# One decoder layer with a mixture of experts: the last expert's rows normalised by themselves and scattered into the output

## What is computed

```
def hierarchical_moe(h, ...):
    ...                      # each token: top-1 group of 8 experts, then top-2 experts inside it
    def expert_block(args):
        xb, e = args
        hid = jax.nn.silu(xb @ w_gate[e]) * (xb @ w_up[e])
        return hid @ w_down[e]
    y = lax.map(expert_block, (x_rows, block_expert)).reshape(R, D)
    y = y * row_w[:, None]
    out = jax.ops.segment_sum(y, row_tok, num_segments=T + 1)[:T]
...
z = ALPHA * h + hierarchical_moe(h, ...)
out = layer_norm(z, ln2_scale, ln2_bias)     # mean and variance over the 2048 channels of a token
```

## Time and profile before

| | us |
|---|---|
| median of 3 executions | 2080.28 (2080.22 to 2081.01) |
| span of the profiled execution, first to last instruction | 2078.8 |
| median less that span | 1.5 |
| PE busy, DVE busy, ACT busy, POOL busy | 1783.7, 980.9, 766.0, 10.1 |

### The profile page before, as it was taken

How to read it: one execution, slowest core, us unless ns; L and a number is a source line. 1 busy time by engine, 2 the same in 40 slices (tenths; PEclk the granted TensorE clock), 3 DMA queues, 4 the chain that set the end, 5 groups by cost and what they waited for, 6 DMA issues and landing times.

```text
span 2078.8 us, 25166 instructions
## 1 busy us (share of the span) xinstructions
PE 1783.7 (86%) x9828; PEld 1156.3 (56%) x9828; DVE 980.9 (47%) x1428; ACT 766.0 (37%) x1332; POOL 10.1 (0%) x26
## 2 busy tenths in 40 slices
PE   9999999999999999999999986667666766666667
PEld 7888888888888888888888541112111211111122
DVE  6454454545444454566565564343443343334334
ACT  5444444344444444354443422222222222222222
POOL 0000000000000000000000000000000000000000
PEclk9999999999999999999999988888888887888889
DMA  7555545455555555467677999999999999999997
GB/s 248 192 176 178 185 153 177 160 187 178 197 183 171 162 180 164 162 189 240 216 274 291 383 428 426 428 430 431 427 430 430 432 429 427 429 430 431 427 429 324
DMA packets 138481, 615.16 MB, mean 296 GB/s; under 512 B 14080, under 2 KB 14752, under 8 KB 117408
## 3 DMA queue, kind: packets, MB, share of 16 engines
q1 hardware_dynamic: 138400, 614.02, 76.8%
HBM read 611.89 MB, written 2.10 MB: 295 GB/s over the span
## 4 chain that ended last, share of the span: by engine, by line
PE 61%; DMA 34%; DVE 2%; issue 1%; ACT 1%; SPq 0%; DVEq 0%; ACTq 0%
DMA W<-in_w_expert_up_dram 21%; PE PS L564 16%; PE PS L566 16%; PE PS L565 16%; DMA W<-in_w_expert_down_dram 13%; PE PS L1119 4%; PE PS L1165 2%; PE PS L866 1%; DVE WL L541 1%; PE PS L910 1%; PE PS L1238 1%; PE PS L890 0%; PE PS L1077 0%; ACT WH L537 0%; PE PS L854 0%
## 5 line engine op out<-in xcount | busy, mean ns | idle before, releaser
L541 DVE TENSOR_TENSOR WL<-RAW,WH 128x1024 fp32r<-128x1024 f32 x384 | 458.1, 1222 | 402.3 <-ACT WH L537 401.1
L537 ACT ACTIVATE WH<-RAW 128x1024 fp32r<-128x1024 f32 x384 | 394.3, 1058 | 251.3 <-PE PS L566 201.9
L564 PE MATMUL PS<-WH,XH 128*128 128x512 f32 x1216 | 485.2, 399 | 1.3 <-DVE WL L541 1.2
L566 PE MATMUL PS<-WH,XL 128*128 128x512 f32 x1216 | 474.6, 390 | 0.0
L565 PE MATMUL PS<-WL,XH 128*128 128x512 f32 x1216 | 473.7, 390 | 0.0
L1119 PE MATMUL PS<-W,XE 128*32 128x512 f32 x2016 | 279.0, 702 | 146.2 <-DMA W<-in_w_expert_up_dram 144.8
L1165 PE MATMUL PS<-W,HT 128*32 128x512 f32 x992 | 170.5, 849 | 132.1 <-DMA W<-in_w_expert_down_dram 132.1
L2150 DVE TENSOR_TENSOR ZACC<-PS,ZACC 128x1024 f32<-128x1024 f32 x116 | 136.6, 1220 | 290.2 <-PE PS L1207 290.2
L1119 PEld LDWEIGHTS PS<-W,XE 128*32 128x32 f32 x2016 | 71.9, 125 | 334.6 <-issue 200.3
L564 PEld LDWEIGHTS PS<-WH,XH 128*128 128x128 f32 x1216 | 228.4, 188 | 50.5 <-DVE WL L541 5.4
L566 PEld LDWEIGHTS PS<-WH,XL 128*128 128x128 f32 x1216 | 228.2, 188 | 49.0
(11 more groups left out here) (309 smaller groups left out, 1500.0 us busy)
## 6 DMA issues: line engine op xcount, KB each, us to landing
RAW<-in_w_in_dram SPq DMA_DIRECT2D x304, 512.0 KB, 4.6
W<-in_w_expert_gate_dram SPq DMA_DIRECT2D x62, 2048.0 KB, 28.6
W<-in_w_expert_up_dram SPq DMA_DIRECT2D x62, 2048.0 KB, 33.1
W<-in_w_expert_down_dram SPq DMA_DIRECT2D x29, 4096.0 KB, 35.2
RAW<-in_w_branch_ret_dram SPq DMA_DIRECT2D x32, 512.0 KB, 4.9
RAW<-in_w_out_dram SPq DMA_DIRECT2D x32, 512.0 KB, 5.7
W<-in_w_expert_down_dram SPq DMA_DIRECT2D x5, 2048.0 KB, 27.8
RAW<-in_w_branch_attn_dram SPq DMA_DIRECT2D x16, 512.0 KB, 5.2
```

Source lines behind the costliest of these rows:

```text
L537: act.activation(WH[:, i % RING], RAW[:, i % RING], ACT.Copy).then_inc(hi_done, 1)
L541: dve.tensor_tensor(WL[:, i % RING], RAW[:, i % RING], WH[:, i % RING].bitcast(F32), ALU.subtract).then_inc(lo_done, 1)
L564: pe.matmul(PS[:, bank + t], hs, wh, start=first and j == 0, stop=False)
L566: mm = pe.matmul(PS[:, bank + t], ls, wh, start=False, stop=end)
```

## The change

It does six things.

1. **Order of the last loads.** `LAST_PLACES` gives the last pieces buffers: down 30 into 0, first half of 31 into 1, second half of 31 into 2, down 31 into 3. Down 30 is now issued ahead of item 31's halves. The broadcast reads of scale and bias go; instead both are read as 32 rows of 128 values (`LN2R`, 8 KB each), early: behind `load_down(2, 2)`, after waits for `table_ready` and `s1_spread` 4.
2. **Order on PE.** Items 29 and 30 are spread and added to `ZACC` as all others. Behind item 30 PE runs `number_slots`, `gather_sums`, `spread_norm2(0)`, `spread_norm2(1)`, first half of item 31, `spread_norm2(2)`, `spread_norm2(3)`, second half of item 31, `spread_compact`, `turn_hidden(31)`, `down_last`, `join_stats`.
3. **All sums but item 31's are normalised and stored.** DVE runs `row_stats` on `ZACC` and `norm_rows(j)` for four quarters of 512 channels, with scale and bias spread by PE into PSUM (`spread_norm2`); SP stores `OB` in two DMAs of 1 MB behind the fourth.
4. **Item 31 stays compact.** `gather_sums` copies the sums of its rows out of `ZACC` into `XE_BANK`; `down_last` accumulates onto them, the row weight being in the hidden values already (`hidden_last`, `WHALF`).
5. **Its LayerNorm** is made on 128 partitions by 512: `bn_stats`, a matmul with `JOIN` that brings the four quarters of a row together, `bn_aggr`, `pow` on POOL and two DVE instructions.
6. **Its rows are scattered**: POOL waits for the stores of step 3 and issues one indirect DMA of 128 rows of 2 KB over them.

The core of the diff (declarations, the branches for `n_more`, and removed functions that the sections above name are left out):

```diff
+LAST_PLACES = {(2, NE - 2): 0, (0, NE - 1): 1, (1, NE - 1): 2, (2, NE - 1): 3}
...
         load_down(2, 2)
+        sp.wait_ge(table_ready, 1)
+        sp.wait_ge(s1_spread, 4)
+        for v, row in ((ln2_scale, 0), (ln2_bias, KD)):
+            sp.dma_start(LN2R[row:row + KD], v.rearrange("l (r n) -> (l r) n", n=P)).then_inc(s2_landed, 16)
...
+        sp.wait_ge(d_used, (NE - 2) * 2)
+        for c in range(2):
+            load_last(2, NE - 2, c)
+        sp.wait_ge(gu_used, (NE - 1) * GU + 2)
+        for c in range(2):
+            load_last(0, NE - 1, c)
         sp.wait_ge(gu_used, NE * GU)
+        for c in range(2):
+            load_last(1, NE - 1, c)
         sp.wait_ge(d_used, (NE - 1) * 2)
+        load_last(2, NE - 1, 0)
...
-        sp.dma_start(S2B[:], ln2_scale.broadcast_to((P, D))).then_inc(s2_landed, 16)
-        sp.dma_start(B2B[:], ln2_bias.broadcast_to((P, D))).then_inc(s2_landed, 16)
+        def store_rows(run):
+            sp.wait_ge(normed, 4 * run + 4)
+            for t in range(TOK):
+                sp.dma_start(out_rows[:, t], OB[:, t]).then_inc(stored, 16)
...
+        def gather_sums():
+            pe.wait_ge(xe_stored, NE * QS)
+            pe.wait_ge(added, (NE - 1) * 4 + 2)
+            for t in range(TOK):
+                for m in range(QD):
+                    pe.matmul(PS[m * ROWS:(m + 1) * ROWS, XE_BANK], SEL[:, t],
+                              ZACC[:, t, m * QC:(m + 1) * QC], start=t == 0, stop=False)
+        def number_slots():
+            pe.wait_ge(slots_ready, 1)
+            for m in range(QD):
+                for t in range(TOK):
+                    mm = pe.matmul(PS[m * ROWS:(m + 1) * ROWS, Y_BANK, 0:1], SEL[:, t], TOKV[:, t:t + 1], ...)
+        def spread_norm2(j, run=0):
+            pe.wait_ge(s2_landed, 32)
+            ...
+            if j >= 2:
+                pe.wait_ge(normed, 4 * run + j - 1)
+            for v in range(2):
+                for r in range(QD):
+                    row = v * KD + j * QD + r
+                    mm = pe.matmul(PS[:, norm_bank(j) + v, r * P:(r + 1) * P],
+                                   RC[0:2 * KD, R_ID + row:R_ID + row + 1].broadcast_to((2 * KD, P)), LN2R[0:2 * KD], ...)
+            mm.then_inc(s2_spread, 1)
+        def spread_compact():
+            pe.wait_ge(normed, 3)
+            for v in range(2):
+                for r in range(QD):
+                    row = v * KD + r
+                    for m in range(QD):
+                        col = R_ID + row + m * QD
+                        mm = pe.matmul(PS[m * ROWS:(m + 1) * ROWS, SPREAD + v, r * P:(r + 1) * P],
+                                       RC[0:2 * KD, col:col + 1].broadcast_to((2 * KD, ROWS)), LN2R[0:2 * KD], ...)
+            mm.then_inc(s2_spread, 1)
...
+        pe.wait_ge(h_ready, NE - 1)
         turn_hidden(NE - 2)
+        for t in range(TOK):
+            spread_rows(NE - 3, t)
+        down(NE - 2, 2, range(KH), halves=True)
+        for t in range(TOK):
+            spread_rows(NE - 2, t)
+        number_slots()
+        gather_sums()
+        spread_norm2(0)
+        spread_norm2(1)
+        gate_up(NE - 1, 3, 0, take(1), last=True)
+        spread_norm2(2)
+        spread_norm2(3)
+        gate_up(NE - 1, 3, 1, take(1), last=True)
+        spread_compact()
         turn_hidden(NE - 1)
         down_last()
+        join_stats()
...
+        def norm_rows(j, run):
+            cols = slice(j * CH, (j + 1) * CH)
+            dve.wait_ge(s2_spread, 5 * run + j + 1)
+            for t in range(TOK):
+                dve.scalar_tensor_tensor(OB[:, t, cols], ZACC[:, t, cols], MV2[:, t, 0:1], PS[:, norm_bank(j)], ...)
+            dve.wait_ge(c_rstd, run + 1)
+            dve.drain()
+            for t in range(TOK):
+                last = dve.scalar_tensor_tensor(OB[:, t, cols], OB[:, t, cols], RSTD2[:, t:t + 1],
+                                                PS[:, norm_bank(j) + 1], ALU.mult, ALU.add)
+            last.then_inc(normed, 1)
...
         row_weights(NE - 2)
+        add_rows(NE - 3, 1)
         row_tokens(NE - 2)
+        y_low(NE - 2)
+        add_rows(NE - 2, 0)
+        row_weights(NE - 1)
+        add_rows(NE - 2, 1)
+        row_tokens(NE - 1)
...
+        row_stats()
+        for j in range(3):
+            norm_rows(j, 0)
+        hidden_last()
+        norm_rows(3, 0)
+        dve.wait_ge(slots_summed, 1)
+        dve.tensor_tensor(IDX[:], PS[:, Y_BANK, 0:1], SLOT[:], ALU.add).then_inc(idx_ready, 1)
+        dve.wait_ge(last_summed, 1)
+        dve.bn_stats(BS3[:], PS[:, XE_BANK])
+        dve.drain()
+        dve.tensor_tensor(BSX[:], BS3[:, None, :].broadcast_to((P, QD, 6)), OWN[:], ALU.mult).then_inc(part_stats, 1)
+        dve.wait_ge(joined, 1)
+        dve.bn_aggr(MV3[:], PS[:, Y_BANK, 8:8 + 6 * QD])
...
+        rstd(MV2[:, :, 1], VE2[:], RSTD2[:], NHF[:], d_stats, 1, c_rstd)
+        pool.wait_ge(last_var, 1)
+        pool.tensor_tensor(RSTD3[:], VE3[:], NHF[:, 0:1], ALU.pow).then_inc(last_rstd, 1)
+        pool.wait_ge(idx_ready, 1)
+        pool.wait_ge(stored, 16 * TOK)
+        pool.wait_ge(last_done, 1)
+        pool.indirect_dma_start(out_slots, bass.IndirectOffsetOnAxis(ap=IDX[:, 0:1], axis=0), LZ[:], None, ...)
```

More of the change, by code:

```diff
@@ L1087, in turn_rows, with gate_up @@
             mm.then_inc(xe_turned, 1)
-        def gate_up(item, k4, q, rows, more=False, gathered_between=None):
+        def gate_up(item, k4, q, rows, more=False, gathered_between=None, last=False):
             by_place = isinstance(item, int) and item < 2 and q == 0
@@ L1093, in gate_up @@
                 pe.wait_ge(xe_stored, item * QS + (q + 1))
-            pair_q = MORE_PAIRS[q] if more else place(q, k4) % PAIRS
+            pair_q = MORE_PAIRS[q] if more else LAST_PLACES[q, item] if last else place(q, k4) % PAIRS
             apart = isinstance(item, int) and item == 0 and q == 1
@@ L1147, in down @@
         def down(item, k4, blocks, first=False, halves=False, more=False):
-            pair_q = MORE_PAIRS[2] if more else place(2, k4) % PAIRS
+            pair_q = MORE_PAIRS[2] if more else LAST_PLACES[2, item] if halves else place(2, k4) % PAIRS
             for b in blocks:
@@ L1198, in spread_rows @@
+        def spread_rows(item, t):
+            if t == 0:
                 pe.wait_ge(g_ready, item + 1)
                 pe.wait_ge(y_act, item + 1)
-            if not onto:
-                pe.wait_ge(added, item * 4 + 2 * (t != first) + 2)
+            pe.wait_ge(added, item * 4 + 2 * t + 2)
             for part, y in ((0, YH), (1, YL)):
-                if t == first and part == 1:
+                if t == 0 and part == 1:
                     pe.wait_ge(y_dve, item + 1)
@@ L1207, in spread_rows @@
                     mm = pe.matmul(PS[:, SPREAD + m], GS[rows, t * P:(t + 1) * P], y[rows, :],
-                                   start=part == 0 and not onto, stop=part == 1 and not onto)
+                                   start=part == 0, stop=part == 1)
                     if part == 1 and m % 2:
                         mm.then_inc(spread, 1)
-        def spread_last(item, t, n, of=(0, 1)):
-            last = item == NE - 1
-            gs, parts = (GSL, (YHL, YLL)) if last else (GS, (YH, YL))
-            for part in of:
-                for m in range(2):
-                    rows = slice((2 * n + m) * ROWS, (2 * n + m + 1) * ROWS)
-                    mm = pe.matmul(PS[:, last_bank(t, n) + m], gs[rows, t * P:(t + 1) * P],
-                                   parts[part][rows, :], start=False, stop=part == 1 and last)
-            if part == 1:
-                mm.then_inc(spread, 1)
         def take(item):
@@ L2152, in add_rows @@
         def add_rows(item, t):
             for n in range(2):
[L2154 to L2171 removed]
+                dve.wait_ge(spread, item * 4 + (2 * t + n + 1))
@@ new lines, in add_rows, with row_stats @@
+                z = ZACC[:, t, n * 2 * QC:(n + 1) * 2 * QC].rearrange("p (m c) -> p m c", m=2)
+                dve.tensor_tensor(z, PS[:, SPREAD + 2 * n:SPREAD + 2 * n + 2], z, ALU.add).then_inc(added, 1)
+        def row_stats():
+            dve.drain()
+            for t in range(TOK):
+                for j in range(4):
+                    dve.bn_stats(BS2[:, t, j], ZACC[:, t, j * CH:(j + 1) * CH])
+            dve.drain()
+            for t in range(TOK):
+                last = dve.bn_aggr(MV2[:, t], BS2[:, t].rearrange("p j s -> p (j s)"))
+            last.then_inc(d_stats, 1)
+            dve.drain()
@@ L2221, in _ @@
         y_low(NE - 3)
-        add_first(NE - 3)
+        add_rows(NE - 3, 0)
         row_weights(NE - 2)
-        hidden(NE - 1)
-        dve.wait_ge(spread, NE * 4 - 8)
+        add_rows(NE - 3, 1)
         row_tokens(NE - 2)
-        row_weights(NE - 1, WROWL)
-        row_tokens(NE - 1, GSL)
-        n_more = dve.value_load(ITAB[0:1, MORE:MORE + 1], min_val=0, max_val=MORE)
-        y_low(NE - 2)
-        y_low(NE - 1, last=True)
-        first_stats(0)
+        y_low(NE - 2)
```

(1 more changed line is left out.)

345 lines of the change are left out of this document (137 added, 208 removed).

## The result

| | before | after |
|---|---|---|
| median, us | 2080.26 (2080.22 to 2081.01, 4 runs) | 2096.78 (2095.57 to 2098.14, 4 runs) |
| span of the profiled execution | 2078.8 | 2095.6 |
| own time of the profiled execution | not shown | 2097.53 |
| last weights landed to the end of the span | 19.3 | 34.6 |

The changed kernel is slower: ratio 1.0075, 95% interval [1.0063, 1.0087], 16.5 us. The spans differ by 16.8 us.

The account below looks back on a forecast made before the run. Weight loads were taken to bound until 2059.5, then a serial PE, DVE and ACT tail; its steps, stores and scatter end the span at 2088.7, plus 1.5 between span and median gives 2090.2 us, range 2085.5 to 2099.0.

Parts of the forecast that it names:

- the clock rival: PE at the lower clock in the tail's new waits: 8.4 us more than the forecast, 2098.6 us; chance 0.17.
- `spread_compact`: PE beside item 31's hidden chain: 64 small instructions at 0.10 each, 6.4 us, ending at 2077.1.
- Loads: Weight stream: same pieces and places of issue, last weights still at 2059.5; cost 0, also for the small reads' wait.
- Item 30: Behind the spreads of item 29: `down(30)` from 2035.0 takes 5.0, then DVE's additions and statistics until 2057.0.
- Gather and two spreads: PE from `slots_ready` at 2050.1: slots, gather and first spread to 2057.2 at mid-clock, second spread to 2059.3.
- First half of item 31: PE behind the second spread: 3.6 us, ending at 2062.9.
- Spreads three and four, second half: PE behind item 31's first half: spreads to 2067.0, item 31's second half to 2070.7.
- Compact LayerNorm: Behind `down_last`: item 31's statistics, join, root and last instruction take 3.7 us, to 2085.4.
- Stores: SP behind `norm_rows(3)` at 2078.2: 2 MB take 2.2 + 5.3 us, landing at 2085.8.
- Scatter: POOL's indirect DMA behind the stores: issued at 2085.9, 2.8 us to landing, ending the span at 2088.7.
- The rival at three small stores: The final scatter costs three small stores, 8.4 us, giving 2095.8 us; chance 0.10.
- The faster rival: The tail shrinks because everything ahead of item 31's down matrix is done while weights land: 2068.7 us; chance 0.05.

Follow-up runs that it names:

- the version with everything early: Changed kernel with item 31 first, idle matmuls, stores by quarters, and DVE work needing no late data moved before item 28's second addition: 2081.12 us, ratio 1.0000.
- The best order tried: The version with everything early, with its last 10 us reordered and one idle matmul before the turn of the hidden state: 2080.46 us, ratio 0.9997.
- the kernel with item 31 ahead: Changed kernel with item 31's own work moved ahead of the LayerNorm of the others: 2088.72 us, ratio 1.0037.

## Why the prediction was right, and where it was off

The direction, the place and the mechanism were as forecast: the weight stream keeps its length, the end moves behind it, and the tail grows because DVE and PE have more to do in an order that puts item 31 behind the LayerNorm of the others. 2096.78 lies in the range, 6.6 us above the forecast of 2090.2 and 1.8 under the 2098.6 of the rival with PE at the lower clock. Of the two, the clock rival, at 0.17, described this kernel better than the forecast, at 0.58.

How near both came is in part luck, as errors of both signs met. `spread_compact` and `number_slots` were priced 2.8 us too high in the forecast (1.6 and 1.2, below) and 4.7 too high in the rival, which had 3.5 for the first. Without them the forecast would be 2087.4, 9.4 us short, and the rival 2093.9.

Point by point, the forecast's time, then the trace's:

- **Loads.** Last weights at 2059.5; measured 2061.0, a step of +1.5. The stream is 1.5 us late already at item 29's down matmuls (start 2021.9, where before had 2020.4), and in the nine kernels of the experiments the stream ended between 2059.2 and 2062.1. The step is within what varies between these profiled executions. The DMA engines stayed full where the new wait for `s1_spread` stands (columns as above, the kernel after):

```profile
1216.00:1228.00 12.00, 7.02 (x49) 2.20 (x49) 8.84 (x12) 0.00 (x0) 0.00 (x0) 0.61 1.00 427
```

- **Item 30.** `down(30)` to start at 2035.0 and take 5.0; it started at 2037.4 and took 5.5. Offset 2.9, of which 1.5 is the stream and 0.5 the longer group. From there DVE's sum was right: `row_tokens(31)` done at 2049.6 by the forecast and 2052.5 in the trace, statistics at 2057.0 and 2059.4.
- **Gather and two spreads.** Forecast 2050.1 to 2059.3, 9.2 us; measured 2052.8 to 2063.8, 11.0. This is the step that failed: "for these three I take the middle of both clocks". Gather and both spreads ran at the lower one throughout: 3.65 and 7.19 us, 3.6 for a spread. The second spread the forecast had at the upper clock. Its 3.4 for a slow one is a mean over the 48 instructions of the earlier trace rows, and in that trace the clock was 0.62 until 1208.0 and 0.50 only from there. The whole would have been longer but for `number_slots`, 0.42 us and not 1.6.
- **First half of item 31.** Forecast 3.6, measured 5.9, for the same reason: +2.3, and the offset is now 6.8 (2069.7 for 2062.9).
- **Spreads three and four, second half.** 7.8 forecast, 7.4 measured; hidden chain 4.8 and 4.9.
- **`spread_compact`.** Forecast 6.4, 1.6 us beyond the hidden chain; measured 1.95 and wholly hidden. 64 instructions by 0.03, not 0.10: the 0.20 for 2 in the earlier trace rows does not scale with the number: here 16 took 0.42 and 64 took 1.95. The same mistake made `number_slots` four times too dear.
- **`down_last`.** 3.6 forecast, 5.0 measured: lower clock again, behind the wait for the hidden values. It took most of what the spread gave back: the end of it is 6.2 late.
- **Compact LayerNorm.** 3.7 and 3.5 (to 2091.4). Between its last DVE instruction and POOL's issue stand 1.0 us that the forecast had as 0.1.
- **Stores.** Issue to landing 7.6 forecast, 6.4 measured. The forecast had them 0.4 us behind the compact rows, the trace has them 0.2 ahead.
- **Scatter.** 2.8 us to landing, as taken from the small store. The rival at three small stores fell. The Trainium skill, page "GPSIMD Engine Reference", section "Instruction dispatch", has about 6 us for the first call of a freshly loaded kernel; no such time shows between the issue and the landing in any of the runs.
- **Around the span.** 1.9 us in the profiled execution (2097.53 less 2095.6), 1.5 forecast.

What the forecast did not weigh is that the lower clock is no price per group: in the kernel after it came after waits and then lay over whatever came next, the gather, two spreads and item 31's first half. Waits are not all of it, though. Three groups were slowed behind 8 to 10 us of work of PE without a wait, with the clock at its upper level just before: item 31's second half in the version with everything early (5.13 us), and its first half in the kernels without the scatter (5.3) and with the loads in the order of before (5.2). In the kernel without the scatter (columns as above):

```profile
2057.00:2060.00 3.00, 3.00 (x31) 2.88 (x33) 2.83 (x6) 0.00 (x0) 0.89 (x2) 1.00 0.75 311
2060.00:2063.50 3.50, 3.50 (x20) 0.91 (x21) 3.35 (x6) 0.00 (x0) 0.00 (x0) 0.51 0.10 42
```

What makes the clock fall in such places stays open.

The forecast knew the case (rival three names the same groups and 5.0 us for each) and argued against it from the mean clock of before, 0.95 and 0.91, "and PE now has more to do in them". But in the 18 us ahead of 2048 it had less: busy for 9.7 (6.22 and 3.46, above), where the kernel before had 12.9.

The faster rival, 2068.7, needs `normed` 4 by 2056.9. The best order tried has it at 2068.2, with everything moved ahead that needs no new weights, and its best run is 2077.05. By the chains of those kernels, what holds it is the way from DVE's additions of items 28 and 29 (until 2033) over `down(30)`, whose weights have landed by then, its additions, item 31's two halves and the gather between them to `down_last`, and the four quarters of the LayerNorm on DVE beside it.

Shown by the runs: the order of the work behind item 30 is worth about 8 us and the lower clock in PE's first waits about 6, each uncertain by some 4 and partly the same time; the scatter costs some 2; the order of the loads is worth 8 in favour of the change; early stores are worth nothing by themselves. Order, idle matmuls and early stores together take away 12.5 of the 16.5 us and the early row weights the rest, and no version tried is faster than before by more than the interval.

## What to carry to other kernels

A split of a final reduction into "all but the last" and "the last" pays only if the first part is finished while the last weights still flow; write down when its last input exists and what its engines must do from there, before anything else. In a queue without waits, the work that the end depends on goes first, and the work that only has to be done some time goes into its waits. After a stretch in which TensorE mostly waits for others, price the next groups at the lower clock, all of them, and try an idle matmul in the wait: here six were worth 6 us, and nine more elsewhere nothing.

## Not expected of the hardware

- TensorE at its lower level for 20.5 us while busy for 78% of them, and in another kernel for all of a group of 6.31 us in 6.82. In a third it went from 1.00 to 0.51 at 2060 in the midst of work without a gap.
- Small matmuls are cheap in number: 64 of 32x32 weights by 128 columns took 1.95 us at the full clock and 3.48 at 0.53, in the kernel with item 31 ahead.
- An indirect DMA from POOL lands 2.8 to 3.9 us after its issue, but is issued 1.0 us after the last semaphore that it waits for (2091.4 to 2092.4 here, 2084.4 to 2085.4 where a store came last).
- Two stores of 1 MB issued together landed 3.9 and 6.0 us later; of 512 KB, issued apart, 2.8 to 4.1 in the median of four.
